# HGRN2 scores in column groups of 32 keys: narrower visits to TensorE, a compact buffer, and a spread to the diagonal by ScalarE

## The reference

```
q, f, inp_v, g = split(h @ w_in)            # 8 heads of 128 channels each
q = silu(q); k = (1 - lb) * sigmoid(-f); log_f = log of the decay per token and channel
# inside a chunk, b = cumsum(log_f):
scores[t, s] = sum_k q[t,k] * k[s,k] * exp(b[t,k] - b[s,k])     for s <= t
o = scores @ v + (q * exp(b)) @ state
state = exp(b_last) * state + (k * exp(b_last - b)).T @ v
```

## Time and profile before

| | |
|---|---|
| median of the runs | 1411.59 us |
| profiled execution, its own time | 1410.82 us |
| its span, first to last instruction | 1409.0 us |
| TensorE busy | 1396.5 us, 99% |
| VectorE busy | 991.5 us, 70% |
| ScalarE busy | 664.0 us, 47% |
| mean granted TensorE clock | 1.000 |

### The profile page before, as it was taken

The page is one execution under the profiler, slowest core; times in us unless marked ns, Lnnn a source line. Parts: engine busy times, 40 slices in busy tenths (PEclk is TensorE's granted clock), DMA queues, the critical chain, the costliest instruction groups (busy, mean ns, idle before and its releaser), DMA issues.

```text
span 1409.0 us, 22510 instructions
## 1 busy us (share of the span) xinstructions
PE 1396.5 (99%) x8351; PEld 1181.6 (84%) x8351; DVE 991.5 (70%) x1730; ACT 664.0 (47%) x1115; POOL 101.1 (7%) x128
## 2 busy tenths in 40 slices
PE   9999999999999999999999999999999999999999
PEld 8888888798887878788878887899888988888878
DVE  7787888764666676766666677667556668787892
ACT  6343434253555555656565666545333433443440
POOL 2122211100000000000000000000000012122210
PEclk9999999999999999999999999999999999999999
DMA  6322223243222222222222221413334132322311
GB/s 187 90 74 77 60 60 91 64 123 105 75 75 75 75 76 75 76 75 75 75 75 76 75 72 34 130 53 104 92 90 111 54 90 61 90 64 75 86 45 60
DMA packets 211679, 113.56 MB, mean 81 GB/s; under 512 B 3743, under 2 KB 209873, under 8 KB 211586
## 3 DMA queue, kind: packets, MB, share of 16 engines
q1 hardware_dynamic: 211202, 112.02, 27.6%
q0 software_dynamic: 384, 0.25, 0.1%
HBM read 110.16 MB, written 2.10 MB: 80 GB/s over the span
## 4 chain that ended last, share of the span: by engine, by line
PE 90%; DVE 6%; ACT 2%; issue 1%; DMA 0%; SPq 0%; DVEq 0%; ACTq 0%
PE ps L602 35%; PE ps L617 35%; PE scores L617 4%; PE scores L784 3%; PE scores L985 2%; PE ps L1016 2%; PE ps L999 2%; PE ps L965 2%; PE ps L813 1%; PE ps L631 1%; DVE scratch L1881 1%; DVE op_lo L1745 1%; PE ps L815 1%; PE scores L802 1%; PE scores L778 1%
## 5 line engine op out<-in xcount | busy, mean ns | idle before, releaser
L617 PE MATMUL ps<-w_hi,op_hi 128*128 128x512 f32 (+1 forms) x880 | 320.0, 364 | 3.0 <-DVE op_lo L1745 1.4
L602 PE MATMUL ps<-op_hi,w_hi 128*128 128x512 f32 (+1 forms) x800 | 319.0, 399 | 0.1
L617 PE MATMUL ps<-w_lo,op_hi 128*128 128x512 f32 (+1 forms) x880 | 309.5, 352 | 0.0
L617 PE MATMUL ps<-w_hi,op_lo 128*128 128x512 f32 (+1 forms) x880 | 308.9, 351 | 0.0
L602 PE MATMUL ps<-op_lo,w_hi 128*128 128x512 f32 (+1 forms) x800 | 305.7, 382 | 0.0
L602 PE MATMUL ps<-op_hi,w_lo 128*128 128x512 f32 (+1 forms) x800 | 304.8, 381 | 0.0
L1687 DVE TENSOR_TENSOR w_lo<-raw,w_hi 128x1024 fp32r<-128x1024 f32 x200 | 239.0, 1219 | 20.1 <-ACT w_hi L1206 20.0
L1206 ACT ACTIVATE w_hi<-raw 128x1024 fp32r<-128x1024 f32 x200 | 202.7, 1052 | 37.2 <-PE ps L617 13.0
L617 PEld LDWEIGHTS ps<-w_hi,op_hi 128*128 128x128 f32 x880 | 166.6, 189 | 27.7 <-issue 6.4
L617 PEld LDWEIGHTS ps<-w_lo,op_hi 128*128 128x128 f32 x880 | 166.4, 189 | 23.0
L577 POOL TENSOR_TENSOR scratch<-scratch 128x256 f32<-128x256 f32 x112 | 94.6, 845 | 1262.1 <-DVE scratch L1862 956.1
(11 more groups left out here) (220 smaller groups left out, 1903.2 us busy)
## 6 DMA issues: line engine op xcount, KB each, us to landing
raw<-in_b_w_in SPq DMA_DIRECT2D x80, 512.0 KB, 3.9
raw<-in_a_w_in SPq DMA_DIRECT2D x64, 512.0 KB, 4.2
raw<-in_c_w_in SPq DMA_DIRECT2D x24, 512.0 KB, 4.8
raw<-in_a_w_out SPq DMA_DIRECT2D x16, 512.0 KB, 3.9
raw<-in_b_w_out SPq DMA_DIRECT2D x8, 512.0 KB, 3.8
raw<-in_c_w_out SPq DMA_DIRECT2D x8, 512.0 KB, 4.6
xt<-in_x SPq DMA_DIRECT2D x4, 512.0 KB, 6.3
y<-in_norm_w SPq DMA_DIRECT2D x3, 512.0 KB, 4.4
```

What stands on the lines that cost most here:

```text
L602: last = nc.tensor.matmul(bank, a, b, start=(k == 0 and p == 0), stop=(k == KT - 1 and p == 2))
L617: last = nc.tensor.matmul(bank, a, b, start=(k == 0 and p == 0), stop=(k == KT - 1 and p == 2))
```

## The change

The keys of a tile are cut into four windows of 32. A window's product uses 32 columns of the array (a column group) and writes 32 PSUM partitions, and only the queries of the same window are computed for the own, pair and m = 2 and m = 8 levels. The results of the four windows lie on top of each other in 32 columns per tile, in a compact buffer `a_sw` (128 x 4 x 32). ScalarE then copies the four windows to their places on the diagonal of `a_sd` (`spread_windows`), and also takes over the three copies of the m = 32 level (`keep_blocks`). The hi and lo split of the products is dropped: own and pairs are computed in fp32 in one visit (`own_and_pairs`). Level m = 32 keeps its 12 products. Every window's last product increments the semaphore by one, so a visit ends with 4, 4, 4 and 3 increments.

```diff
-                    def scores(g):
-                        ...
-                        nc.tensor.matmul(to, ones_sq, qk_hi[:, cols], start=True, stop=False)
-                        last = nc.tensor.matmul(to, ones_sq, qk_lo[:, cols], start=False, stop=True)
-                        last.then_inc(g_ready, 1)
+                    def own_and_pairs():
+                        pe.wait_ge(qk_done, h + 1)
+                        if later:
+                            pe.wait_ge(st_step, h * 3)
+                        for at, wide in ((0, S), (S, S // 2)):
+                            products = a_qk[:, at:at + wide].rearrange("p (t w c) -> p w t c", t=TT, w=WINDOWS)
+                            for w in range(WINDOWS):
+                                to = score[0][w * WINDOW:(w + 1) * WINDOW, at // 4:(at + wide) // 4]
+                                last = nc.tensor.matmul(to, a_ones, products[:, w], start=True, stop=True)
+                                if at:
+                                    last.then_inc(g_ready, 1)
                     def quad_scores(r):
                         m = QUADS[r]
+                        bank = score[(r + 1) % 2]
                         pe.wait_ge(far_done, h * 6 + 2 * r + 2)
                         pe.wait_ge(keys_moved, h * LEVELS + 2 * r + 1)
-                        pe.wait_ge(sd_done, h * KEPT + 2 + 3 * r)
+                        if r == 0 and later:
+                            pe.wait_ge(sd_spread, h * SPREAD)
+                        if r:
+                            pe.wait_ge(sd_done, h * KEPT + (2, 5)[r - 1])
                         for t in range(TT):
-                            ...
-                            of = a_qq[:, prev, 0:2, tile].rearrange("p x (h c) -> p x h c", c=4 * m)[:, :, :, m:]
-                            last = nc.tensor.matmul(scores2[:, t * 256:t * 256 + 192], a_k[:, prev, tile], of, ...)
-                        last.then_inc(g_ready, 1)
+                            for w in range(WINDOWS if m < WINDOW else WINDOWS - 1):
+                                ...
+                                if m < WINDOW:
+                                    of = a_qq[:, prev, 0:2, keys].rearrange("p x (h c) -> p x h c", c=4 * m)[:, :, :, m:]
+                                    to = bank[rows, t * 48:t * 48 + 48]
+                                else:
+                                    of = a_qq[:, prev, 0:3 - w, keys.start + m:keys.stop + m]
+                                    to = bank[rows, t * 96:t * 96 + (3 - w) * m]
+                                last = nc.tensor.matmul(to, a_k[:, prev, keys], of, start=True, stop=True)
+                                if t == TT - 1:
+                                    last.then_inc(g_ready, 1)
                     def values():
-                        pe.wait_ge(sd_done, h * KEPT + KEPT)
+                        pe.wait_ge(sd_spread, h * SPREAD + SPREAD)
+                    def spread_windows():
+                        act.wait_ge(sd_done, h * KEPT + KEPT)
+                        if later:
+                            act.wait_ge(o_ready, h)
+                        for w in range(WINDOWS):
+                            of = slice(w * WINDOW, (w + 1) * WINDOW)
+                            last = nc.scalar.activation(a_sd[of, :, of], a_sw[of], ACT.Copy)
+                        last.then_inc(sd_spread, 1)
+                    def keep_blocks():
+                        act.wait_ge(g_ready, h * G_STEPS + G_STEPS)
+                        for w in range(WINDOWS - 1):
+                            ...
+                            last = nc.scalar.activation(a_sd[keys, :, keys.stop:], of, ACT.Copy)
+                        last.then_inc(sd_spread, 1)
-                    if proj:                                     # ScalarE
-                        act.wait_ge(qk_done, i + (H0 + 1))
-                        ...
-                        nc.scalar.activation(qk_hi, a_qk, ACT.Copy).then_inc(qk_hi_done, 1)
-                    def split_products():                        # VectorE
-                        dve.wait_ge(qk_hi_done, i + (H0 + 1))
-                        nc.vector.tensor_tensor(qk_lo, a_qk, qk_hi.bitcast(F32), ALU.subtract).then_inc(qk_lo_done, 1)
```

More of the change, by code:

```diff
@@ L47 @@
 QUADS = (2, 8, 32)
[L48 to L51, removed]
+WINDOW = 32
+WINDOWS = P // WINDOW
+VISIT_ENDS = (WINDOWS, 2 * WINDOWS, 3 * WINDOWS, 4 * WINDOWS - 1)
+G_STEPS = VISIT_ENDS[-1]
+KEPT = 2 + 3 * (len(QUADS) - 1)
+SPREAD = 2
+QUAD_MASK = 3 * WINDOW // 2
+MASKS = WINDOW + WINDOW // 2 + QUAD_MASK * (len(QUADS) - 1)
 SMALL_CONSTANTS = 10
@@ L200, in build @@
         a_qk, at = carve(at, S + S // 2)
-        qk_hi, qk_lo = (w[:, 2, 0:6].rearrange("p k c -> p (k c)") for w in (w_hi, w_lo))
-        ones_sq = w_hi[:, 5, 0]
+        a_sw, at = carve(at, TT, WINDOW)
+        a_ones, at = carve(at, WINDOW)
         a_mask = sb("a_mask", [P, MASKS], U8)
@@ L773, in quad_scores @@
                         for t in range(TT):
[L774 to L781, removed]
@@ L782, in quad_scores @@
-                            tile = slice(t * P, (t + 1) * P)
-                            of = a_qq[:, prev, 0:2, tile].rearrange("p x (h c) -> p x h c", c=4 * m)[:, :, :, m:]
-                            last = nc.tensor.matmul(scores2[:, t * 256:t * 256 + 192], a_k[:, prev, tile], of,
-                                                    start=True, stop=True)
-                        last.then_inc(g_ready, 1)
+                            for w in range(WINDOWS if m < WINDOW else WINDOWS - 1):
+                                rows = slice(w * WINDOW, (w + 1) * WINDOW)
+                                keys = slice(t * P + w * WINDOW, t * P + (w + 1) * WINDOW)
+                                if m < WINDOW:
[7 more added lines that the diff above has]
+                                    last.then_inc(g_ready, 1)
@@ L877, in body @@
                     if mix and not proj:
-                        scores(0)
-                        scores(1)
+                        own_and_pairs()
                         turn_v()
@@ L908, in body @@
                     if mix:
-                        for g in range(2):
-                            steps[g] = [lambda g=g: scores(g)]
-                        steps[1].append(turn_v)
+                        steps[0] = [own_and_pairs]
+                        steps[1] = [turn_v]
                         for r, at in ((0, 4), (1, 11), (2, 17)):
@@ L1345, in body @@
                         root(h - 1)
-                        act.wait_ge(g_ready, h * G_STEPS + 2)
                         split_out(n, (4,))
+                        spread_windows()
+                        keep_blocks()
                     if proj:
@@ L1368, in body @@
                         nc.scalar.activation(a_sig[:, 0], acc[1][:], ACT.Sigmoid).then_inc(q_act, 1)
+                        if mix:
+                            keep_blocks()
                         if last_proj:
@@ L1853, in products @@
                         dve.wait_ge(q_done, i + (H0 + 1))
-                        if not (static(i) and i + H0 == 0):
-                            dve.wait_ge(qk_lo_done, i + H0)
                         nc.vector.tensor_tensor(a_qk[:, 0:S], q, k, ALU.mult)
@@ L1898, in far_queries @@
                         moved(2 * r + 1)
-                        to = slice(1, 3) if r == len(QUADS) - 1 else slice(2, 4)
+                        to = slice(2, 4) if m < WINDOW else slice(1, 3)
                         nc.vector.tensor_tensor(far[:, :, to], q[:, :, 2:4],
@@ L1985, in body @@
                         dve.wait_ge(o_ready, h)
+                        spread_before()
                         taken(0)
                         keep_own()
-                        taken(1)
                         kept(1)
```

87 lines of the change are left out of this document (40 added, 47 removed).

## The result

The changed kernel takes 1394.44 us (median of four runs, 1391.97 to 1398.18) beside 1411.91 for the kernel before in the same runs (1411.56 to 1412.49): a ratio of 0.9878, 95% interval 0.9853 to 0.9903. It is faster by 1.2%, the side and the range forecast, but 6.4 us above the forecast of 1388.0, and its runs lie 6.2 us apart where those of the kernel before lie 0.9 apart. It is also outside the 1383 to 1391 that the prediction gave its likeliest case. The profiled execution took 1398.18, span 1396.2.

A forecast was written before the change was run, and what follows sets the result against it. TensorE, busy 1396.5 of 1409.0 us, was taken as the bound: 14 steady heads (7 per layer) save 19.0 and two tails 4.6, together 23.6 off 1410.82, giving 1387.2; plus 0.8 for the median, 1388.0. Range 1383 to 1397.

The forecast's parts named there:

- likeliest case: Whole kernel: groups run at their own full pace, time 1388.0 us, own range 1383 to 1391, chance 0.62.
- Column groups run side by side: Narrow visits on TensorE: each lasts as long as its longest group, 0.33 us, plus 0.32; quad visit 0.65 against 1.31.
- Four groups in turn: Rival for TensorE's narrow visits: groups alternate, quad visit 1.64 us, kernel 1434, head over 31; chance 0.03.
- starts at 25 ns: Rival for TensorE's narrow visits: pass starts paced at 25 ns, quad visit 1.12 us, kernel 1403; chance 0.08.
- 17 ns: Rival for TensorE's narrow visits: pass starts paced at 17 ns, quad visit 0.86 us, kernel 1394; chance 0.20.
- The fixed part: Every column-group visit on TensorE: 0.32 us for going in and out, bounded between 0.18 and 0.32.
- the prediction's own pricing: TensorE visit cost: start of last projection pass before to start of second pass behind, less two normal distances of 0.227 us.
- increments hold TensorE: Rival in steady heads: 10 more semaphore increments at 26 ns cost 0.26 us a head, kernel 1392; no separate chance.
- Other engines in a steady head: VectorE's shorter copies and ScalarE's added ones, about 2.3 us likely, stay off TensorE's path: worth nothing.
- the cover: Steady head: 4 us between ScalarE's delayed hi halves and their reader, VectorE's lo halves at 122.02.
- The tails: Two layer tails, set by VectorE's chain: shift 1.9 us plus 0.38 ahead of L824, 2.3 each, 4.6 together.
- another stall: Anywhere in the kernel: an unforeseen stall or a larger fixed part, together given chance 0.07; no size stated.

The follow-up runs named there:

- the merged kernel: Own and pairs moved to just ahead of quad visit 0, against the changed kernel with early lo half of y and 64 ScalarE waits: 1383.37 us, ratio 0.9801.
- moved code: Changed kernel plus only 64 ScalarE waits on a long-set semaphore (32 instructions) ahead of layer B's loop: 1391.57 us, ratio 0.9859.

## Why the prediction was right, and what it missed

**Column groups run side by side: right.** 32 passes of 48 columns in four groups started within 0.34 us, in rounds 43 ns apart, which are the 0.041 of the forecast 8 x 0.041 = 0.33. Four groups in turn would have made a head of over 31 us, starts at 25 ns one of 29.3, at 17 ns one of 28.75; it was 28.45, at each of the 12 distances from one steady head to the next. The Trainium skill, TensorE: Matmul & The Clock Gate, "Wait — 56ns, not 53.3ns?", has starts never closer than about 25 ns; these traces disagree, with 11 ns over a whole visit of 32 passes and 12 over one of 64.

**The fixed part: a little too small.** It was taken as 0.32 and came out at 0.68 - 0.33 = 0.35 by the prediction's own pricing (0.34 if the 0.34 that the starts took is set against it), in the three narrow visits (the m = 32 visit kept its 0.98). Each narrow quad visit saved 0.63, not 0.66, and own and pairs 0.02, not 0.04. This mis-sized term makes 1.24 per head in place of 1.36: 14 x 1.24 = 17.4 us in place of 19.0, so 1.6 us of the 6.4. That the fixed part is per visit, and not per pass or increment, the merged kernel shows: one visit fewer, 0.30 less. That increments hold TensorE is out: 33 more cost nothing. The Trainium skill, same page, "The cost: per-tile semaphore tail", gives 26 ns for each, as a delay of the tail; here it stays off TensorE's path in the steady heads, and 12 more in visit 0 made the chain to visit 1 0.25 us longer in the tails, 21 ns each.

**Other engines in a steady head: right.** ScalarE's splits of the next weights ran at 113.14 to 115.15, inside the cover, and TensorE has no idle piece there. They were expected at 115.8 to 117.8, but visit 2, for which the copies ahead of them wait, now starts at 111.00 in place of 113.80; moved back to VectorE, the copies changed nothing (28.45).

**The tails: right in mechanism and, at full clock, in size; the clock was missed.** VectorE's chain from the first move to the last ran 2.45 us (237.70 to 240.15) in place of 3.32, 0.87 less where 0.75 was forecast, so the wait ahead of visit 1 is 0.36 and not 0.7; and the 0.38 in front of the transposes of the mixed output (L824) is gone. The prediction said that the wait ahead of the first output product would grow, and priced it as idle time. It did not ask what a longer idle piece does to the clock behind it. In some executions TensorE falls to 1.2 GHz two microseconds later, 1.6 us at each place, which takes most of a tail's gain; in others of the same kernel it doesn't.

**What the sum left out: a third place.** The sum has two kinds of places, steady heads and tails, and takes it for granted that nothing else changes. A third, in a layer that the change doesn't touch, cost 1.8 to 3.3 us of TensorE idle: ScalarE's back branch in layer B. The changed program has 37 more ScalarE instructions ahead of that loop; with 17 more (the copies back on VectorE), 69 or 101 the stall is gone. That the number of instructions ahead of the loop decides is shown by adding nothing but such instructions. The profile names no releaser, but its DMA records have, in every stalled profile and in no other, a transfer of instructions inside the stall, and ScalarE goes on 1.7 to 1.9 us behind its start. Why code is fetched there at this position and not at the four others is open.

**The account.** The kernel without either stall (moved code, filled idle time) takes 1390.3. Its profile spans 1388.4 us, 20.6 less than before, where 23.6 were forecast. The steady heads give 17.4 and the tails, at full clock, 4.7; the added waits take 0.5 of this back. Of the 1.0 us left, 0.7 lies ahead of the first quad visit (43.55 in place of 42.84). That start varies between executions, 42.98 to 44.37 in the twelve profiles of the changed kernels, and there is only one profile of the kernel before, so this part is open, as are the last 0.3. The changed kernel itself is slower than this one by the clock in the tails, 1.3 us (1391.57 against 1390.3), and by the branch with the clock behind it. Set against the kernel before in its own runs, it gained 17.5 us the first time and 15.7 the second, the moved code 19.8, so the branch costs 2.3 to 4.1, or 0.5 more, since the moved code pays for its waits.

**What was luck.** The side was right by the mechanism, and so were the heads and tails. That the whole range held was in part luck: it reached to 1397 for the sake of the 17 ns rival, whose 1394 is nearly the time measured, and that rival is out by the head of 28.45. The range was not drawn for a stall in layer B and a falling clock, which took the time there; the nearest it came is "another stall", with a share of 0.07 together with a larger fixed part.

## What to carry to other kernels

Narrow fp32 products of 32 output rows pack four to one in column groups, at a fixed 0.3 us per visit: put as many of them as the dependences allow into one visit. An idle piece on TensorE can cost more than its length, by the clock behind it: pull what ends it forward (one split moved into idle time of VectorE brought 3.5 us here, 1391.57 to 1388.11: two times 1.0 as wait, the rest by the clock, 0.999 on average before and 1.000 after). Compare the places that a change doesn't touch, too; a few instructions more on an engine can slow a loop elsewhere, and the DMA queues that carry instructions are worth a look where a wait has no releaser.

## What the runs showed of the hardware

- In four column groups TensorE started 32 passes of 48 columns in 0.34 us: 7 ns from group to group, 43 ns from one pass of a group to its next. With two products of the same group following each other, 64 starts took 0.78 us, 12 ns each.
- Going into column groups and out costs 0.30 to 0.35 us a visit of 16, 24 or 32 fp32 passes: 0.32 to 0.35 by the pricing of single visits, 0.30 by leaving one out.
- After 1.68 us of TensorE idle the granted clock behind it was 0.53 in one execution and 1.00 in another of the same kernel; with the branch stall away its mean over the span was 0.999 in all four runs with this idle time and 1.000 in all four with passes in it, and 1.000 in all eight runs with 0.68 us of idle time. A fall costs 1.6 us.
- The back branch of one and the same loop on ScalarE took 0.24 to 0.26 us in the kernels where the stall is absent (the one before, the copies back on VectorE, and the five with added waits) and 3.5 to 5.0 us in six profiles of the others, depending on how many instructions stand ahead of it. A transfer of 8192 bytes of instructions starts inside the stall in all six, 1.67 to 1.90 us ahead of ScalarE's next instruction, and none in the other seven.
- 33 more semaphore increments a head left TensorE's pace as it was (28.45 us); 12 of them reached a waiting VectorE 0.25 us later.
